# Two feed-forward chunks per down projection: six products per accumulation group in a two-layer decoder step

## The reference

```python
def conv_ffn(h, prev, w_up, conv_w, conv_b, w_down):
    up = h @ w_up
    a, b = up[..., :D_FF], up[..., D_FF:]
    ext = jnp.concatenate([prev, a], axis=1)
    c = conv(ext, conv_w) + conv_b          # three taps along the rows, per channel
    return (silu(c) * b) @ w_down, ext[:, -2:]
x = x + conv_ffn(rms_norm(x, norm2_g), ...)
```

## Time and profile before

| | us |
|---|---|
| median of 3 runs | 3089.33 |
| lowest, highest | 3088.89, 3091.76 |
| profiled execution, first to last instruction | 3088.1 |
| chunk loop, layer 0 | 767 to 1511 |
| last chunk and tile stage, layer 0 | 1511 to 1543 |
| chunk loop and last chunk, layer 1 | 2290 to 3054 |

### The profile page before, as it was taken

How to read it: one execution, slowest core, us unless ns; L and a number is a source line. 1 busy time by engine, 2 the same in 40 slices (tenths; PEclk the granted TensorE clock), 3 DMA queues, 4 the chain that set the end, 5 groups by cost and what they waited for, 6 DMA issues and landing times.

```text
span 3088.1 us, 45465 instructions
## 1 busy us (share of the span) xinstructions
PE 2837.5 (92%) x16776; PEld 2587.2 (84%) x16776; DVE 1545.4 (50%) x1931; ACT 785.2 (25%) x1516; POOL 932.2 (30%) x768
## 2 busy tenths in 40 slices
PE   5889898988999999999988989888999999999996
PEld 4768686867999999999876867777789999999996
DVE  5746464555443444444575463647454444443435
ACT  3221313134222222222233131222332222222222
POOL 4624333244212212221254252525242121212220
PEclk7999898988999999999988998889889999999998
DMA  3422222121111111111113222321111111111111
GB/s 119 125 69 66 89 69 82 49 82 38 46 41 41 55 48 41 41 41 47 52 51 98 68 91 68 99 62 58 52 49 41 41 41 51 52 41 41 41 41 55
DMA packets 70800, 184.00 MB, mean 60 GB/s; under 512 B 8014, under 2 KB 28936, under 8 KB 70552
## 3 DMA queue, kind: packets, MB, share of 16 engines
q1 hardware_dynamic: 33352, 105.95, 10.1%
q0 software_dynamic: 18496, 67.58, 7.0%
q10 hardware_dynamic: 18848, 8.96, 1.0%
HBM read 169.27 MB, written 13.64 MB: 59 GB/s over the span
## 4 chain that ended last, share of the span: by engine, by line
PE 51%; issue 29%; POOL 10%; DVE 6%; ACT 2%; SPq 1%; POOLq 0%; ACTq 0%; DMA 0%; DVEq 0%
PE bank L921 22%; PE bank L950 9%; PE bank L1097 4%; POOL w_lo L498 4%; PE bank L1085 4%; PE bank L967 3%; PE bank L939 3%; PE bank L1132 3%; POOL act_lo L525 2%; PE bank L1112 1%; POOL page L562 1%; DVE rot L1412 1%; ACT scratch L764 1%; DVE scratch L1474 1%; POOL page L584 1%
## 5 line engine op out<-in xcount | busy, mean ns | idle before, releaser
L498 POOL TENSOR_TENSOR w_lo<-w_raw,w_hi 128x1024 fp32r<-128x1024 f32 x180 | 441.5, 2454 | 1474.2 <-ACT w_hi L630 1474.0
L1375 DVE TENSOR_TENSOR resid<-bank,resid 128x1032 f32<-128x1032 f32 x400 | 489.9, 1231 | 431.0 <-PE bank L950 431.0
L921 PE MATMUL bank<-act_hi,w_hi 128*128 128x344 f32 x2640 | 570.3, 324 | 0.0
L921 PE MATMUL bank<-act_hi,w_lo 128*128 128x344 f32 x2640 | 560.5, 320 | 0.0
L921 PE MATMUL bank<-act_lo,w_hi 128*128 128x344 f32 x2640 | 556.5, 319 | 0.0
L921 PEld LDWEIGHTS bank<-act_hi,w_hi 128*128 128x128 f32 x2640 | 439.6, 188 | 9.3 <-issue 0.4
L921 PEld LDWEIGHTS bank<-act_hi,w_lo 128*128 128x128 f32 x2640 | 446.3, 189 | 0.0
L921 PEld LDWEIGHTS bank<-act_lo,w_hi 128*128 128x128 f32 x2640 | 439.6, 188 | 0.0
L950 PE MATMUL bank<-mix_hi,w_hi 128*128 128x344 f32 x1200 | 291.5, 352 | 36.3 <-DVE resid L1375 36.3
L950 PE MATMUL bank<-mix_lo,w_hi 128*128 128x344 f32 x1200 | 259.3, 325 | 0.0
L950 PE MATMUL bank<-mix_hi,w_lo 128*128 128x344 f32 x1200 | 258.1, 324 | 0.0
(11 more groups left out here) (235 smaller groups left out, 3661.9 us busy)
## 6 DMA issues: line engine op xcount, KB each, us to landing
w_raw<-in_w_up SPq DMA_DIRECT2D x88, 512.0 KB, 3.5
w_raw<-in_w_down SPq DMA_DIRECT2D x44, 512.0 KB, 3.4
w_raw<-in_w_in SPq DMA_DIRECT2D x32, 512.0 KB, 3.4
w_raw<-in_w_out SPq DMA_DIRECT2D x16, 512.0 KB, 3.4
out<-v_tok ACTq DMA_DIRECT2D x16, 512.0 KB, 3.4
page<-in_x_prompt SPq DMA_DIRECT2D x4, 512.0 KB, 9.6
out<-page SPq DMA_DIRECT2D x4, 512.0 KB
out<-rows_out ACTq DMA_DIRECT2D x104, 4.0 KB
```

What stands on the lines that cost most here:

```text
L498: pool.tensor_tensor(w_lo[:, slot, :], w_raw[:, slot, :], w_hi[:, slot, :].bitcast(F32), ALU.subtract).then_inc(w_lo_done, 1)
L921: ins = pe.matmul(g[:, t, 0:TW], w[:, slot, k * P:(k + 1) * P], x[:, k, t * TW:(t + 1) * TW], start=(k == 0 and n_ == 0), stop=(k == KC - ...
L1375: dve.tensor_tensor(tiles(resid[:, m, :]), grp3(u[0]), tiles(resid[:, m, :]), ALU.add).then_inc(g_free[u[0]], 1)
```

## The change

Chunks are taken in pairs. TensorE's loop has 10 turns per layer and holds, in this order, B(2i), A(2i+1), B(2i+1), A(2i+2), and one down projection for both chunks: each PSUM group gets 18 matmuls, six products in three tiles, and is added once. The odd chunk's gate has buffers of its own, `odd_hi` and `odd_lo`. The last pair goes tile by tile, with twelve matmuls per PSUM group. Slots, the loading order and the orders of ScalarE and VectorE follow. The split of the next layer's unit 1 waits for the last use of the layer before. SBUF for the two new buffers comes with a smaller scratch for GpSimd's DMA descriptors.

```diff
-G_FFN = 2 + KC
+FP = FC // 2
+G_PAIR = 4 + KC
...
-G_LAYER = G0_FFN + G_FFN * (FC - 1) + 1 + TILE_USES
+G_LAYER = G0_FFN + G_PAIR * (FP - 1) + 3 + TILE_USES
...
+        odd_hi = sb("odd_hi", [P, T], F32R)
+        odd_lo = sb("odd_lo", [P, T], F32R)
...
+        gates_hi, gates_lo = (mix_hi, odd_hi), (mix_lo, odd_lo)
...
-                with sp.Fori(0, FC - 1) as i:
-                    load_a(i + 1, f0 + i * 3 + 2, 2)
-                    load_state(i + 1)
-                    load_d(i, f0 + i * 3 + 3, 0)
-                    load_b(i + 1, f0 + i * 3 + 4, 1)
-                load_d(FC - 1, f0 + 3 * FC - 1, 2)
+                with sp.Fori(0, FP - 1) as i:
+                    n = f0 + i * 6
+                    load_a(i * 2 + 1, n + 2, 2)
+                    load_state(i * 2 + 1)
+                    load_b(i * 2 + 1, n + 3, 0)
+                    load_a(i * 2 + 2, n + 4, 1)
+                    load_state(i * 2 + 2)
+                    load_d(i * 2, n + 5, 2)
+                    load_d(i * 2 + 1, n + 6, 0)
+                    load_b(i * 2 + 2, n + 7, 1)
...
-                split_hi(l, 0, 1, 0, (1, l * (G_LAYER // 2)))
+                split_hi(l, 0, 1, 0, use(G_SETUP // 2 + l * (G_LAYER // 2), -1))
...
+                def first_half(i):
+
+                    split_hi(l, i, U_FFN0 + 3, 2, use_ffn(l, i, -1))
+                    store_conv(i * 2)
+                    gate_hi(0, use_ffn(l, i, 0))
+                    split_hi(l, i, U_FFN0 + 4, 2, use_ffn(l, i, 0))
+                    evacuate_a(i * 2 + 1, use_ffn(l, i, 1))
+                    split_hi(l, i, U_FFN0 + 5, 2, use_ffn(l, i, 1))
+                    silu(i * 2 + 1)
+                    store_conv(i * 2 + 1)
+                    gate_hi(1, use_ffn(l, i, 2))
+
+                with act.Fori(0, FP - 1) as i:
+                    first_half(i)
+                    split_hi(l, i, U_FFN0 + 6, 2, use_ffn(l, i, 2))
+                    evacuate_a(i * 2 + 2, use_ffn(l, i, 3))
+                    split_hi(l, i, U_FFN0 + 7, 2, use_ffn(l, i, 3))
+                    silu(i * 2 + 2)
+                    split_hi(l, i, U_FFN0 + 8, 2, use_ffn(l, i, G_PAIR - 1))
+                first_half(FP - 1)
...
+            def terms(slots):
+
+                return [(w[:, slot], x) for odd, slot in enumerate(slots)
+                        for w, x in ((w_hi, gates_hi[odd]), (w_hi, gates_lo[odd]), (w_lo, gates_hi[odd]))]
...
-                with pe.Fori(0, FC - 1) as i:
-                    up_unit(f0 + i * 3 + 1, 1, use_ffn(l, i, 0))
-                    new_rows(i)
-                    up_unit(f0 + i * 3 + 2, 2, use_ffn(l, i, 1))
-                    state_rows(i + 1)
-                    down(i, f0 + i * 3 + 3, 0, 2)
+                with pe.Fori(0, FP - 1) as i:
+                    three_units(i)
+                    up_unit(f0 + i * 6 + 4, 1, use_ffn(l, i, 3))
+                    state_rows(i * 2 + 2)
+                    pe.wait_ge(g_lo_done, l * FC + i * 2 + 2)
+                    unit_ready(f0 + i * 6 + 6)
+                    for m in range(KC):
+                        down_part((2, 0), m, use_ffn(l, i, 4 + m))
+                three_units(FP - 1)
...
                 for i in range(NT):
-                    down_tile(2, i, lambda j: use_ffn(l, FC - 1, 1 + j))
+                    down_tile((1, 2), i, lambda j: use_ffn(l, FP - 1, 3 + j))
...
-                with dve.Fori(0, FC - 1) as i:
-                    gate_b(i, use_ffn(l, i, 0))
-                    add_rows(lambda m: use_ffn(l, i, 2 + m))
-                    taps(i + 1)
+                def two_gates(i):
+
+                    gate_b(i * 2, 0, use_ffn(l, i, 0))
+                    taps(i * 2 + 1)
+                    gate_b(i * 2 + 1, 1, use_ffn(l, i, 2))
+
+                with dve.Fori(0, FP - 1) as i:
+                    two_gates(i)
+                    add_rows(lambda m: use_ffn(l, i, 4 + m))
+                    taps(i * 2 + 2)
...
-    nc = bacc.Bacc("TRN2", target_bir_lowering=False, num_devices=1)
+    nc = bacc.Bacc("TRN2", target_bir_lowering=False, num_devices=1, dynamic_dma_scratch_size=4096)
```

More of the change, by code:

```diff
@@ L364, in use_ffn @@
         def use_ffn(l, i, j):
-            return use(G_SETUP // 2 + l * (G_LAYER // 2) + i * (G_FFN // 2), G0_FFN + j)
+            return use(G_SETUP // 2 + l * (G_LAYER // 2) + i * (G_PAIR // 2), G0_FFN + j)
         def use_layer(l, j):
@@ L472, in _ @@
                 load_state(0)
-                with sp.Fori(0, FC - 1) as i:
-                    load_a(i + 1, f0 + i * 3 + 2, 2)
-                    load_state(i + 1)
-                    load_d(i, f0 + i * 3 + 3, 0)
-                    load_b(i + 1, f0 + i * 3 + 4, 1)
-                load_d(FC - 1, f0 + 3 * FC - 1, 2)
+                with sp.Fori(0, FP - 1) as i:
[8 more added lines that the diff above has]
+                    load_b(i * 2 + 2, n + 7, 1)
+                n = f0 + 6 * (FP - 1)
+                load_a(FC - 1, n + 2, 2)
+                load_state(FC - 1)
+                load_b(FC - 1, n + 3, 0)
+                load_d(FC - 2, n + 4, 1)
+                load_d(FC - 1, n + 5, 2)
             for t in range(QT_N + 1):
@@ L855, in store_conv, with gate_hi @@
                                       ).then_inc(conv_out_s, 16)
-                def gate_hi(c, u):
+                def gate_hi(odd, u):
                     released(act, u)
-                    act.activation(mix_hi[:, :], gate[:, :], ACT.Copy).then_inc(g_hi_done, 1)
+                    act.activation(gates_hi[odd][:, :], gate[:, :], ACT.Copy).then_inc(g_hi_done, 1)
                 split_hi(l, 0, U_FFN0 + 2, 0, use_layer(l, G0_A0 - 1))
@@ L942, in up_unit_by_tile, with down_part, down_tile @@
                 ins.then_inc(g_full[u[0]], 1)
-            def down_part(slot, m, u):
+            def terms(slots):
+                return [(w[:, slot], x) for odd, slot in enumerate(slots)
+                        for w, x in ((w_hi, gates_hi[odd]), (w_hi, gates_lo[odd]), (w_lo, gates_hi[odd]))]
+            def down_part(slots, m, u):
                 wait_free(u)
                 g = grp(u[0])
-                for n_, (w, x) in enumerate(((w_hi, mix_hi), (w_hi, mix_lo), (w_lo, mix_hi))):
+                products = terms(slots)
+                for n_, (w, x) in enumerate(products):
                     for t in range(NT):
-                        ins = pe.matmul(g[:, t, 0:TW], w[:, slot, m * P:(m + 1) * P], x[:, t * TW:(t + 1) * TW],
-                                        start=(n_ == 0), stop=(n_ == 2))
+                        ins = pe.matmul(g[:, t, 0:TW], w[:, m * P:(m + 1) * P], x[:, t * TW:(t + 1) * TW],
+                                        start=(n_ == 0), stop=(n_ == len(products) - 1))
                 ins.then_inc(g_full[u[0]], 1)
[L954 to L959, removed]
+            def down_tile(slots, i, uses):
+                products = terms(slots)
                 for j in range(PAIRS):
@@ L965, in down_tile @@
                         m = 2 * j + a
-                        for n_, (w, x) in enumerate(((w_hi, mix_hi), (w_hi, mix_lo), (w_lo, mix_hi))):
-                            ins = pe.matmul(grp(u[0])[:, a, 0:TW], w[:, slot, m * P:(m + 1) * P], x[:, tile_of(i)],
-                                            start=(n_ == 0), stop=(n_ == 2))
+                        for n_, (w, x) in enumerate(products):
+                            ins = pe.matmul(grp(u[0])[:, a, 0:TW], w[:, m * P:(m + 1) * P], x[:, tile_of(i)],
+                                            start=(n_ == 0), stop=(n_ == len(products) - 1))
                     ins.then_inc(g_full[u[0]], 1)
@@ L1064, in _ @@
                     for m in range(KC):
-                        down_part(1, m, ug(("wg", m)))
+                        down_part((1,), m, ug(("wg", m)))
                         if m == 0:
@@ L1178, in _ @@
                             pe.wait_ge(t_free, ta(("o", QT_N)) + 2)
-                        down_tile(2, i, lambda j: ug(("wh", j)))
+                        down_tile((2,), i, lambda j: ug(("wh", j)))
                 norm(l * 2 + 1, l * T_LAYER + T0_NORM2)
@@ L1194, in new_rows, with three_units @@
                     pe.transpose(t_bank[0:26, 0:P], ext_tail, ident).then_inc(t_full, 1)
-                def down(c, n, slot, first_use):
-                    pe.wait_ge(g_lo_done, l * FC + c + 1)
-                    down_unit(n, slot, lambda m: use_ffn(l, c, first_use + m))
+                def three_units(i):
+                    n = f0 + i * 6
+                    up_unit(n + 1, 1, use_ffn(l, i, 0))
+                    new_rows(i * 2)
+                    up_unit(n + 2, 2, use_ffn(l, i, 1))
+                    state_rows(i * 2 + 1)
+                    up_unit(n + 3, 0, use_ffn(l, i, 2))
+                    new_rows(i * 2 + 1)
                 state_rows(0)
                 up_unit_by_tile(f0, 0, use_layer(l, G0_A0), l * 2 + 1)
-                with pe.Fori(0, FC - 1) as i:
-                    up_unit(f0 + i * 3 + 1, 1, use_ffn(l, i, 0))
```

(16 more changed lines are left out.)

## The result

The changed kernel takes 3063.21 us in the median of 4 runs (3056.57 to 3065.33), the kernel before, run beside it, 3090.55 (3088.89 to 3094.43): a ratio of 0.9906, 95% interval 0.9892 to 0.9920. 3061.7 had been forecast, with 3055 to 3080 as the range.

The account below looks back on a forecast made before the run. TensorE, busy 92%, was taken to bound the kernel, with VectorE's additions pacing the down stages. The terms -27.6 - 4.2 + 4.2 = -27.6 us gave 3060.5 profiled, 3061.7 us median, range 3055 to 3080.

Parts of the forecast that it names:

- VectorE paces the down stage by 0.08 us per group: Chunk loop's down projections: VectorE's turn of 1.49 us exceeds nine matmuls' 1.42, by 0.08 us, eight times per chunk.
- Pairs, -27.6 us: Down projections of ten pairs in each of two layers: 22.74 us per pair against 24.12, 1.38 less, together -27.6 us.
- The last pair in tiles, -4.2: Last pair's down projection, in groups of twelve matmuls: 24.3 us against 26.41, 2.1 saved per layer, -4.2 us.
- The wait at the start of the layer, +4.2: Between the layers: ScalarE's split waits for the last group ahead of the squares, so the norm starts 4.2 us later.
- the jump's 3 us: TensorE's jump back to the layer's start: 3.03 us after the last matmul before, now hidden under the longer wait.
- The weights' chain, nothing: Next pair's second up unit: low part ready 8.7 us after the down stage, 2.7 us of room, no cost.
- a late chain: Next pair's second up unit: if its weights came 4 us late, the cost would be 1.3 x 18 = 23 us.
- The jump back, nothing: TensorE's chunk loop: the pair's body of 4.7 instruction packets stays on the chip, so its jumps cost zero.
- The sum: Whole kernel: -27.6 - 4.2 + 4.2 = -27.6 us, so 3060.5 profiled and 3061.7 in the median.

Follow-up runs that it names:

- shorter additions: The kernel before, with VectorE's additions in the chunk loop cut to two of the three column tiles: 3063.63 us, ratio 0.9911.
- the later split: The changed kernel, with unit 1's split behind the squares of tiles 0 and 1 and its low part behind tile 1's pair sums: 3055.07 us, ratio 0.9879.
- 7.1 packets: The kernel before, with TensorE's loop taking three chunks per turn, seven turns per layer: 3090.79 us, ratio 0.9997.
- the body of 9.4: The changed kernel, with TensorE's loop taking two pairs per turn, five turns per layer: 3069.74 us, ratio 0.9927 to the kernel before.

## Why the prediction was right, step by step

*VectorE paces the down stage by 0.08 us per group.* Right, and shown from both sides: groups of 18 (the change) and shorter additions on groups of nine each bring the turn to the matmuls' own time, and what went in the second case is 0.07 to 0.11 us at the switch of groups alone.

*Pairs, -27.6 us.* Right in mechanism, a little small. A down projection for two chunks takes 22.69 us (forecast 22.74). A pair takes 69.24 us against 2 x 35.40, which is 1.56 less where 1.38 had been forecast: 0.05 of the rest lies in the down stage, 0.13 in the up stages, above all in the one behind it (11.38 in place of 11.49), whose first matmuls no longer wait for an addition; shorter additions do the same there (11.39). Over 20 pairs that is 31.2 us.

*The last pair in tiles, -4.2.* The tile stage takes 24.5 us where 24.3 had been worked out. With 26.41 before, 1.9 us per layer: -3.8.

*The wait at the start of the layer, +4.2.* Measured 7.09 - 3.34 = +3.75. The order of events was as forecast row by row: split, low part, pair sums, TensorE's sums. The sum had two small slips: 7.1 - 3.03 is 4.07, not 4.2, and the two spans were counted from different points. From the end of the last matmul both are 6.77 and 3.03, from its start 7.09 and 3.34: +3.75. The prediction also had the jump's 3 us lie under the longer wait unchanged. In fact the pairs had made the jump itself cheaper. In the kernel before, the last group of the tile stage waited for an addition (it ended at 1541.16, the group began at 1541.21), and the jump's packet came at 1542.33, behind the last matmul's start. With groups of twelve the bank was free 0.83 us ahead (1526.85, 1527.68), and the packet came at 1528.00, 1.43 us ahead of the last matmul. All four kernels with groups of six have it 0.2 to 0.7 us after that start, all six with groups of twelve 0.8 to 1.5 us before it. Under the new wait this brought nothing, until the later split took the wait away. That the additions are what held the stream back fits these times, but no run tested it alone.

*The weights' chain, nothing.* Right. The rows of ScalarE and GpSimd after the pair of above, answering:

```profile
845.97 1.06 ACT L857 ACTIVATE rot<-scratch 128x1024 f32<-128x1024 f32 x1 [22.53 <-DVE scratch L1571]
...
848.16 4.76 POOL L512 TENSOR_TENSOR w_lo<-w_raw,w_hi 128x1024 fp32r<-128x1024 f32 x2 [22.24 <-ACT w_hi L644]
...
853.21 0.72 PE L946 MATMUL bank<-act_hi,w_hi 128*128 128x344 f32 x3
```

The down stage ended at 841.83. The first of the two low parts is done at about 850.6 (half of 4.76 after 848.16), 8.7 us later as forecast, and TensorE begins the unit at 853.21, with 2.7 us of room. (The 23 us that the prediction put on a late chain counted 18 places; there are ten per layer, so 26.)

*The jump back, nothing.* Right. From 850 to 1480 us the changed kernel's queues are:

```profile
q1 hardware_dynamic: 8640, 29.51, 14.1%
q10 hardware_dynamic: 684, 0.18, 0.1%
q8 instruction: 1, 0.02, 0.0%
```

The one packet falls at the loop's end. The body of 4.7 packets stays. Of the Trainium skill's two statements ("Runtime: NRT & Kernel Launch", "Instruction fetch mechanics"), the window of two pages is refuted for TensorE by bodies of 2.4, 4.7 and 7.1 packets, whose jumps back fetch nothing. The store of 128 KiB filled in blocks of 16 KiB, which makes eight, agrees with them, with the heads (9 packets in every turn) and with the body of 9.4, but for that one's first two jumps.

*The sum.* The terms as measured give -31.2 - 3.8 + 3.75 = -31.3 us, the medians -27.3 and -26.5. The forecast of -27.6 lies nearer to the medians than the corrected terms do, and that is chance: the missing 4 us are no part of the FFN stages, which repeat within 0.3 us in the two profiles of this kernel and within 1.2 over the five profiles with one pair per turn. The profiles put such differences into the heads. Of the twenty stages "heads and norm" in the ten profiles, those that take 689 to 690 us have TensorE at the 1.2 GHz level for 143 to 144 us, and those that take 694.3 us and more for 155 to 159. The change doesn't lengthen them: the heads of both layers take 1383.7 us in the mean of the four profiles with single chunks and 1384.8 in that of the six with pairs. That the scatter has this source in the runs without a profile too is likely but wasn't shown. The interval, 0.9892 to 0.9920, holds 3088.1 - 31.3 (0.9899) as well.

## What to carry to other kernels

An engine that is idle half of the time can still pace one stage: compare its whole turn on a buffer (release, work, release) with what the other engine does on the other buffer, by start times, and lengthen the group until the turn is covered. When a buffer's last reader moves, look at whose queue the new wait stands in and what is behind it; here moving one split behind work that was ready was worth another 5 us. Count the instructions of a hardware loop before making its body longer.

## What was not expected

- TensorE's stream held a loop body of 7.1 instruction packets (some 1320 matmuls and weight loads) without fetching it again, and didn't hold one of 9.4 (some 1744) beyond its first two jumps in one layer, and not at all in the other.
- The price of a jump to code that isn't on the chip depends on how early TensorE's stream meets it: 2.6 to 3.2 us of idle time in the heads, where the packet is asked for behind the last matmul's start; 1.4 to 1.8 us behind 144 down matmuls without a wait, where it is asked for some 2.7 us ahead.
- The step between matmuls of the same shape is 0.1567 us in a down group of 18 and 0.1579 in an up unit and in a down group of nine, and in the up unit the order of the products doesn't matter for it.
